# Rows by pair in pieces: the first tile's later batches and the second tile's parts moved into the second tile's routing

## The chip, the core and the metric

The kernel is one program on one core of a Trainium2 chip. The metric is device time in microseconds from one launch. The core has a tensor engine (PE), a vector engine (DVE), a scalar engine (ACT), a GpSimd engine (POOL, which here issues the gathers) and a sync engine (SP, which loads weights). Each runs its own list of instructions in the order in which they are written, and they meet at semaphores. Sixteen DMA engines move all data between HBM and SBUF.

## What is computed

A transformer block on x (256 tokens, width 1024), then two layers of a second kind on x and on a context of 256 tokens. What matters here is the feed-forward part of the second kind, which picks 16 experts per head for each token (8 heads, so 128 rows of each table per token):

```python
def chunk(hc):                                  # 128 tokens
    q = (hc @ w_query).reshape(128, 8, 2, 64)
    s = jnp.einsum('chpd,hpnd->chpn', q, sub_keys)
    s_top, i_top = lax.top_k(s, 16)             # 16 of 128, for each half
    cand = (s_top[:, :, 0, :, None] + s_top[:, :, 1, None, :]).reshape(128, 8, 256)
    best, pos = lax.top_k(cand, 16)
    eid = take_along_axis(cand_id, pos)         # 128 expert ids a token
    gate = softmax(best)
    u = jnp.take(u_tab, eid, axis=0)            # 128 rows of 1024 floats a token
    act = gelu(jnp.einsum('chkd,cd->chk', u, hc)) * gate
    v = jnp.take(v_tab, eid, axis=0)
    return jnp.einsum('chk,chkd->cd', act, v)
```

It runs for the context and x of the first layer and for x of the second: six tiles of 128 tokens.

## The kernel before

**Tiles.** Tiles 0 and 1 are the context (tag c0), 2 and 3 are x of layer 0 (x0), 4 and 5 x of layer 1 (x1). A tile is *routed*: `scores` (8 matmuls for each half, line 820) gives the scores, DVE finds the best in the steps "top 0" to "top 3", "pairs 0" to "pairs 3", "keys 0" to "keys 3" (`sixteen_best`, lines 1403 to 1415, and `route`), and the ids and gates are turned by PE (lines 836, 837) and copied (`experts`, semaphore `idx_ready`).

**Visits.** The tokens of a routed tile are worked off in pairs, 64 a tile, 384 in all, each by a `visit`. POOL gathers 128 rows of u and of v for both tokens of the pair (four indirect DMAs of half a MB, lines 2128 and 2138; three pairs of buffers each, u up to two pairs ahead). PE spreads the two tokens' own rows over all partitions (`spread`, four matmuls, line 425), DVE multiplies and sums (`dot`, two instructions, line 1035), ACT takes the gelu, DVE multiplies by the gate (line 1044), and two visits later PE adds the v rows (`outputs`, line 439). The spread needs the tile's rows in the form `hs`: a batch for eight pairs.

**Rows by pair.** To get `hs`, `hidden` transposes the tile's 128x1024 activations on PE (line 786), ACT and DVE split them into three bf16 parts (`hp1`, `hp2`, `hp3`; DVE lines 1438 and 1443, semaphore `parts_ready`), and `rows_by_pair` selects by matmul (line 799): eight batches, 12 matmuls each into one PSUM bank, which ACT copies to `hs`. The parts of one tile lie in one place, so those of the next wait until the rows before are made.

**What sets the order.** The order is written out by hand, the same on every engine. Work between visits is followed by `beat(key, us)`, which adds `us` to an account and puts in a visit for each 6.8 in it (PACE); `stream(key, upto)` puts in visits up to a number. The first stream of visits (0 to 255) opens after tile 0 is routed and runs through tile 1's routing, the whole first block, layer 0 of x, and ends in a tail of bare visits; the second (256 to 383) opens after tile 4's routing. While a stream is open, five of the eight PSUM banks belong to it and three are left for all other work. In `route_second("c0", BESIDE)` the first block's norm and first products (in1 0 and in1 1, line 403, 32 matmuls and two visits' beats each) stand between tile 1's routing steps.

`route_first` makes all eight batches of its tile after its routing. `route_second("c0")` then makes tile 1's parts and its eight batches, then its scores, then routes it; `route_second("x0")` and `("x1")` take the scores, route, and make parts and batches after the routing. In x0, two visits (`stream("tile 1 done")`) stand ahead of `route_second`.

## Time and profile before

| | us |
|---|---|
| median of 3 runs | 3563.71 |
| lowest, highest | 3562.61, 3567.37 |
| the profiled execution: its time | 3573.93 |
| its span (first to last instruction) | 3572.2 |
| busy: PE, DVE, POOL, ACT | 2369.1, 1678.6, 1485.1, 561.1 |
| moved by DMA | 1047.22 MB, mean 293 GB/s |

The profiled execution takes 10.2 us more than the median; times below are on its clock, from the start of its span. Stages: context mixer and tile 0's routing up to 448 us, tile 1's routing with the first products to 581, the first block to about 1160, layer 0 of x to 1545, tile 2's routing to 1608, tile 3's to 1746, the front of the layer-1 context and the tail of bare visits to 2410, layer 1 of x to 2740, tile 4's and 5's routing to 2903, the last tail to the end. Rows are read so: a row of the timeline has start, duration, engine, line, operation, output and input, how many instructions it merges, and in brackets how long the engine had been idle before and what it waited for.

### The profile page before, as it was taken

What the parts mean: (1) busy time and instruction counts of PE and PEld (TensorE: products, weight loads), DVE (VectorE), ACT (ScalarE), POOL (GpSimd) and SP (SyncE); (2) the same over time, 40 slices, a digit from 0 to 9 for tenths busy, and PEclk for the clock granted to TensorE, in tenths of its full rate; (3) what the DMA queues carried; (4) which work ended last, traced back from release to release, by engine and by line L of the source; (5) the groups of instructions that cost most, each with busy time, mean ns of one, the idle gap of its engine ahead of it and who ended that gap; (6) DMA issues with size and microseconds to landing.
All of it is one profiled execution on the core that took longest, in us unless ns stands there. A gap on an engine that the chain in (4) does not pass through costs nothing.

```text
span 3572.2 us, 36970 instructions
## 1 busy us (share of the span) xinstructions
PE 2369.1 (66%) x12540; PEld 1286.0 (36%) x12540; DVE 1678.6 (47%) x4368; ACT 561.1 (16%) x1180; POOL 1485.1 (42%) x1577
## 2 busy tenths in 40 slices
PE   6799657898998889964564444448996344444444
PEld 4477434366776446651110000006686110000000
DVE  2511655634334674376654444445415654444443
ACT  2310231401111252021220000003312110000000
POOL 1000034444444444405556666650000456666665
PEclk9899878799999979986665555558998555555555
DMA  8866669899999878938799999991140789999998
GB/s 291 320 241 231 229 223 327 297 358 364 371 361 362 292 274 320 367 121 292 281 344 361 355 352 355 360 340 61 54 170 25 249 315 354 356 355 360 356 354 322
DMA packets 325915, 1047.22 MB, mean 293 GB/s; under 512 B 27424, under 2 KB 38752, under 8 KB 325728
## 3 DMA queue, kind: packets, MB, share of 16 engines
q0 software_dynamic: 240192, 880.90, 66.4%
q1 hardware_dynamic: 85536, 163.95, 13.1%
q8 instruction: 101, 1.65, 0.2%
q14 instruction: 86, 0.70, 0.1%
HBM read 1043.70 MB, written 1.05 MB: 292 GB/s over the span
## 4 chain that ended last, share of the span: by engine, by line
PE 38%; DVE 20%; another core or an unknown queue 16%; issue 14%; DMA 4%; ACT 4%; PEld 3%; POOL 1%; DVEq 0%; PEldq 0%; ACTq 0%; POOLq 0%
PE ps L403 23%; DVE UV L1035 9%; PE ps L439 4%; PE ps L425 2%; PEld ps L403 2%; ACT arena L1661 2%; PE ps L395 2%; DMA UV<-in_v_tab,idxT 2%; PE ps L799 1%; DVE arena L1409 1%; DVE arena L1415 1%; DVE arena L1406 1%; DVE arena L1412 1%; PE ps L570 1%
## 5 line engine op out<-in xcount | busy, mean ns | idle before, releaser
L1035 DVE SCALAR_TENSOR_TENSOR UV<-ps,UV 128x1024 f32<-128x1024 f32 x768 | 909.7, 1222 | 1033.2 <-remote 594.2
L2128 POOL DMA_INDIRECT UV<-in_u_tab,idxT x768 | 724.4, 943 | 1296.7 <-DVE UV L1035 571.7
L2138 POOL DMA_INDIRECT UV<-in_v_tab,idxT x768 | 728.4, 948 | 395.0 <-issue 199.7
L439 PE MATMUL ps<-UV,acts 128*32 128x512 f32 x3072 | 637.9, 916 | 284.1 <-DMA UV<-in_v_tab,idxT 235.1
L403 PE MATMUL ps<-H,W 128*128 128x256 f32 (+2 forms) x3296 | 672.5, 365 | 44.5 <-ACT H L1661 22.8
L403 PEld LDWEIGHTS ps<-H,W 128*128 128x128 f32 (+1 forms) x3296 | 577.1, 195 | 159.9 <-issue 83.6
L425 PE MATMUL ps<-hs,selb 32*128 32x512 bf16 x1536 | 209.9, 532 | 610.1 <-DVE UV L1035 442.2
L425 PEld LDWEIGHTS ps<-hs,selb 32*128 32x128 bf16 x1536 | 42.3, 97 | 1068.2 <-DVE UV L1035 636.9
L403 PE MATMUL ps<-arena,W 128*128 128x256 f32 (+1 forms) x1632 | 373.0, 386 | 25.3 <-issue 13.7
L403 PEld LDWEIGHTS ps<-arena,W 128*128 128x128 f32 (+1 forms) x1632 | 305.3, 190 | 108.0 <-issue 57.7
L1661 ACT ACTIVATE gel<-dots 128x2 f32<-128x2 f32 x384 | 77.2, 202 | 1453.9 <-DVE UV L1035 883.4
L1661 ACT ACTIVATE arena<-ps 128x512 f32<-128x512 f32 (+6 forms) x288 | 150.6, 527 | 817.7 <-PE ps L403 646.5
L439 PEld LDWEIGHTS ps<-UV,acts 128*32 128x32 f32 x3072 | 76.0, 130 | 437.6 <-issue 435.4
L2108 POOL DMA_DIRECT2D UV<-in_w_mod x18 | 16.1, 899 | 254.9 <-ACTq L1713 254.0
L1184 DVE SCALAR_TENSOR_TENSOR arena<-arena,ps 128x512 f32<-128x512 f32 x44 | 30.2, 688 | 183.4 <-PE ps L403 179.2
L1661 ACT ACT_TABLE_LOAD x76 | 97.5, 1283 | 45.3 <-PE ps L570 24.4
L528 PE MATMUL ps<-UV,gateT 128*32 128x512 f32 x432 | 73.0, 647 | 26.5 <-DMA UV<-in_w_mod 14.3
L1262 DVE SCALAR_TENSOR_TENSOR arena<-arena,vec 128x256 f32<-128x256 f32 x180 | 79.3, 482 | 4.8 <-DVE arena L1016 0.7
L799 PE MATMUL ps<-arena,place 128*32 128x512 bf16 x576 | 51.9, 521 | 36.7 <-DVE arena L1443 20.1
L1044 DVE TENSOR_TENSOR acts<-gel,gateT 128x2 f32<-128x2 f32 x384 | 60.6, 158 | 6.3 <-ACT gel L1661 5.1
L1035 DVE DVE_READ_ACCUMULATOR UV<-ps,UV 128x1 f32 x768 | 63.5, 83 | 0.0
L1661 ACT ACTIVATE arena<-arena 128x512 f32<-128x512 f32 (+5 forms) x42 | 46.7, 1112 | 90.2 <-DVEq L1440 49.9
(198 smaller groups left out, 1639.1 us busy)
## 6 DMA issues: line engine op xcount, KB each, us to landing
W<-in_w_in SPq DMA_DIRECT2D x30, 2048.0 KB
UV<-in_w_mod POOLq DMA_DIRECT2D x18, 2048.0 KB, 12.8
W<-in_w_ff SPq DMA_DIRECT2D x16, 2048.0 KB
UV<-in_w_ada POOLq DMA_DIRECT2D x9, 2048.0 KB, 12.0
W<-in_w_out SPq DMA_DIRECT2D x8, 2048.0 KB
W<-in_w_mod POOLq DMA_DIRECT2D x6, 2048.0 KB, 17.6
W<-in_w_query SPq DMA_DIRECT2D x6, 2048.0 KB
UV<-in_u_tab,idxT POOLq DMA_INDIRECT x768
```

The lines of the kernel that those rows point to most:

```text
L395: last = mm(o, lhs[k], rhs[k], start=(k == 0), stop=(k == n - 1))
L403: last = mm(o, w[:, k, col:col + m], src[:, k, c], start=(k == 0), stop=(k == kt - 1))
L425: last = mm(ps[:, HB + r, :], selb[q, u:u + 1].to_broadcast([32, P]), hs[q, n % 2, s, :], start=True, stop=True)
L439: last = mm(ps[q:q + GROUP, YB, :], acts[:, tok % SLOTS, GROUP - 1 - r:2 * GROUP - 1 - r], Vs[:, tok % SLOTS, hf * 512:(hf + 1) * 512], st ...
L528: last = mm(o[q:q + 32, :], cond32[:, 4 * kh + kk, :], w[j][:, 4 * kh + kk, :], start=(kk == 0), stop=(kk == 3))
L799: last = mm(o[32 * r:32 * r + 32, :], place[:, at:at + 32], part[:, hf * 512:(hf + 1) * 512], start=(i == 0), stop=(i == 2))
L1035: dve.scalar_tensor_tensor(out=Us[:, j, :], in0=ps[:, b:b + 2, :].rearrange("p a b -> p (a b)"), scalar=1.0, in1=Us[:, j, :], op0=MUL, op1 ...
L1044: dve.tensor_tensor(out=acts[:, j:j + 2, GROUP - 1], in0=gel[:, j:j + 2], in1=gateT[:, n % 2, t:t + 2], op=MUL).then_inc(sem("acts"), 1)
L1262: last = dve.scalar_tensor_tensor(out=a, in0=u, scalar=wt, in1=a, op0=MUL, op1=ADD)
L1661: return act.activation(o, i, f, **kw)
L2128: pool.indirect_dma_start(Us[:, j, :], None, A["u_tab"], off).then_inc(sem(f"u_arrived{j}"), 16)
L2138: pool.indirect_dma_start(Vs[:, j, :], None, A["v_tab"], off).then_inc(sem(f"v_arrived{j}"), 16)
```

## The change

1. `rows_by_pair(n, batches)` makes only the batches that are named. `route_first` makes none any more. `route_second` makes batch 0 of the first tile, then scores 0 of the second, batch 1, scores 1, and batches 2 to 7 after step "top 0" of the second tile's routing.
2. In x0 the two visits "tile 1 done" stand behind these scores and no more ahead of the first tile's rows.
3. In c0 the second tile's `hidden` (transposes and parts) stands after "top 1", its rows after "top 2", behind the first block's norm, which moves from "top 0" to "top 2"; the first products in1 0 move from "top 2" to "top 3".
4. `rows_after(n)` makes the second tile's batches two at a time with a beat of 3.4 after each two; in x0 and x1 it takes the place of the eight batches in one piece.
5. The signals that the head sums are full are given ahead of the last beat in `mixer_front`; the instruction that carries the signal is the same.

Matmuls, copies and DMAs are the same in number and size.

```diff
@@ PE, the front of the mixer
                     if i:
                         last = key_sums(i - 1)
+                    if i == 4:
+                        full(last, (tag, "hsum"))
                     beat((tag, "hp", i), 2.5)
-                full(last, (tag, "hsum"))
...
@@ PE
-            def rows_by_pair(n):
+            def rows_by_pair(n, batches):
 
                 pe.wait_ge(sem("parts_ready"), n + 1)
-                for s in range(PAIRS // BATCH):
+                for s in batches:
...
                 routes(n)
                 for a in range(2):
                     give_back(("ht", n, a))
-                rows_by_pair(n)
 
             def route_second(tag, beside={}):
 
                 n = TILE_OF[tag] + 1
-                if tag == "c0":
-                    hidden(n, bank)
-                    rows_by_pair(n)
                 for a in range(2):
+                    rows_by_pair(n - 1, [a])
                     scores(n, a)
-                routes(n, beside)
+                if tag == "x0":
+                    stream("tile 1 done", max(seen[0], 2 * PAIRS + 2))
+                routes(n, {"top 0": [lambda: rows_by_pair(n - 1, range(2, 8))], **beside})
                 if tag != "c0":
                     hidden(n, bank)
-                    rows_by_pair(n)
+                    rows_after(n)
+
+            def rows_after(n):
+
+                for s in range(0, 8, 2):
+                    rows_by_pair(n, [s, s + 1])
+                    beat(("rows", n, s), 3.4)
...
-            BESIDE = {"top 0": [lambda: norm("f", "n1")], "top 2": [lambda: first_products(0)], "pairs 2": [lambda: first_products(1)]}
+            BESIDE = {"top 1": [lambda: hidden(1, bank)], "top 2": [lambda: norm("f", "n1"), lambda: rows_after(1)],
+                      "top 3": [lambda: first_products(0)], "pairs 2": [lambda: first_products(1)]}
...
             stream("tile 0 done", max(seen[0], PAIRS + 2))
             route_first("x0")
-            stream("tile 1 done", max(seen[0], 2 * PAIRS + 2))
             route_second("x0")
@@ DVE (ACT has the same moves)
-            BESIDE = {"top 0": [first_norm], "top 2": [lambda: first_products(0)], "pairs 2": [lambda: first_products(1)]}
+            BESIDE = {"top 1": [lambda: hidden_last(1)], "top 2": [first_norm, lambda: rows_after(1)],
+                      "top 3": [lambda: first_products(0)], "pairs 2": [lambda: first_products(1)]}
```

**PE, after tile 0 is routed.** Lines 836 and 837 (838, 839 after) turn its ids and gates; line 799 (801) makes rows, line 820 (822) the scores of tile 1, line 786 (788) the transposes, line 425 spreads, line 439 outputs, line 554 the norm's sum. Before:

```order
L837 MATMUL ps<-ident,arena 128x128
L799 MATMUL ps<-arena,place 32x512 x96
L786 MATMUL ps<-ident,H 128x128 x8
L799 MATMUL ps<-arena,place 32x512 x96
L820 MATMUL ps<-arena 128x128 x8
L425 MATMUL ps<-hs,selb 128x512 x4
L820 MATMUL ps<-arena 128x128 x8
L425 MATMUL ps<-hs,selb 128x512 x4
L554 MATMUL ps<-H,ones 128x256 x8
```

After:

```order
L839 MATMUL ps<-ident,arena 128x128
L801 MATMUL ps<-arena,place 32x512 x12
L822 MATMUL ps<-arena 128x128 x8
L801 MATMUL ps<-arena,place 32x512 x12
L822 MATMUL ps<-arena 128x128 x8
L425 MATMUL ps<-hs,selb 128x512 x4
L801 MATMUL ps<-arena,place 32x512 x72
L788 MATMUL ps<-ident,H 128x128 x8
L425 MATMUL ps<-hs,selb 128x512 x8
L439 MATMUL ps<-UV,acts 32x512 x4
L554 MATMUL ps<-H,ones 128x256 x8
```

The scores of tile 1 had 192 row matmuls ahead of them and now have 12; the first spread now has 24 ahead. Tile 1's own 96 row matmuls come behind the norm, in two blocks of 48 with a visit behind each.

**DVE, the same place.** Lines 1438 and 1443 (1445, 1450 after) make a tile's parts, 1403 to 1415 (1410 to 1422) are a "top" step, 1035 (1042) the dots of a visit. Before:

```order
L1438 TENSOR_TENSOR arena<-ps,arena 128x512 x2
L1443 TENSOR_TENSOR arena<-arena 128x1024
L1438 TENSOR_TENSOR arena<-ps,arena 128x512 x2
L1443 TENSOR_TENSOR arena<-arena 128x1024
L1035 SCALAR_TENSOR_TENSOR UV,dots<-ps,UV 128x1024 x2
L1403 MAX arena<-arena 128x8 x4
```

After:

```order
L1445 TENSOR_TENSOR arena<-ps,arena 128x512 x2
L1450 TENSOR_TENSOR arena<-arena 128x1024
L1410 MAX arena<-arena 128x8 x4
L1413 MAX_INDEX arena<-arena 128x8 x4
L1416 MATCH_REPLACE arena<-arena 128x128 x4
L1419 MAX arena<-arena 128x8 x4
L1422 MAX_INDEX arena<-arena 128x8 x4
L1042 SCALAR_TENSOR_TENSOR UV,dots<-ps,UV 128x1024 x2
```

Tile 1's first step stood behind its parts and the first visit, and stands ahead of both now. Its parts come two steps later.

**PE, after tile 5 is routed.** The same lines; the stream of visits goes on behind. Before:

```order
L786 MATMUL ps<-ident,H 128x128 x8
L425 MATMUL ps<-hs,selb 128x512 x4
L439 MATMUL ps<-UV,acts 32x512 x4
L799 MATMUL ps<-arena,place 32x512 x96
L425 MATMUL ps<-hs,selb 128x512 x4
```

After:

```order
L788 MATMUL ps<-ident,H 128x128 x8
L425 MATMUL ps<-hs,selb 128x512 x4
L439 MATMUL ps<-UV,acts 32x512 x4
L801 MATMUL ps<-arena,place 32x512 x24
L425 MATMUL ps<-hs,selb 128x512 x4
L439 MATMUL ps<-UV,acts 32x512 x4
L801 MATMUL ps<-arena,place 32x512 x48
L425 MATMUL ps<-hs,selb 128x512 x4
L439 MATMUL ps<-UV,acts 32x512 x4
L801 MATMUL ps<-arena,place 32x512 x24
```

Two visits now stand inside the block of rows. After tile 3 it is two blocks of 48 with a visit behind each. Of the 256 visits of the first stream, numbers 0 to 15 (before 0 to 13) now fall before tile 1 is routed, each later place in the first block and in layer 0 of x has a number higher by two, and the last two such places (the last `out` product and the norm behind it) have none; 150 visits (before 149) are done when the front of the layer-1 context begins.

## Rows read from the trace of the kernel before

**Rows 1.** Windows of long stretches: busy us (instructions) of each engine, PEclk, DMA share, GB/s
```profile
700.00:1140.00 440.00, 416.73 (x2163) 304.29 (x2162) 166.38 (x348) 44.79 (x111) 198.52 (x212) 0.98 0.98 363
...
1630.00:1744.00 114.00, 44.07 (x228) 8.09 (x232) 86.84 (x315) 11.41 (x25) 68.13 (x72) 0.52 0.90 326
...
2799.00:2903.00 104.00, 40.28 (x194) 6.93 (x194) 82.83 (x298) 10.52 (x21) 60.60 (x63) 0.50 0.87 314
...
2930.00:3572.00 642.00, 273.75 (x1312) 38.33 (x1312) 268.58 (x568) 24.05 (x111) 399.40 (x426) 0.51 0.94 352
```
**Rows 2.** The same view of five short stretches, at the blocks of rows
```profile
464.00:482.00 18.00, 10.91 (x136) 5.53 (x136) 5.02 (x8) 9.44 (x16) 0.37 (x1) 0.81 0.01 4
...
1624.00:1632.00 8.00, 4.47 (x43) 2.04 (x44) 6.18 (x13) 3.33 (x7) 3.75 (x4) 0.97 0.46 137
...
1762.00:1776.00 14.00, 10.13 (x80) 4.51 (x68) 4.85 (x8) 7.82 (x13) 1.88 (x2) 0.87 0.13 41
...
2790.00:2799.00 9.00, 4.40 (x40) 3.03 (x40) 3.67 (x12) 4.81 (x8) 1.35 (x2) 0.61 0.08 31
...
2916.00:2925.00 9.00, 7.44 (x60) 1.71 (x52) 3.96 (x8) 3.32 (x7) 1.88 (x2) 0.68 0.30 102
```
**Rows 3.** Timeline after tile 0's routing: PE, DVE and POOL (columns: section on the profile)
```profile
452.78 6.40 PE L799 MATMUL ps<-arena,place 128*32 128x512 bf16 x72 [5.00 <-DVE arena L1443]
...
469.76 7.61 PE L799 MATMUL ps<-arena,place 128*32 128x512 bf16 x96 [5.06 <-DVE arena L1443]
...
465.61 0.69 DVE L1438 TENSOR_TENSOR arena<-ps,arena 128x512 f32<-128x512 f32 x1 [12.88 <-ACT arena L1661]
...
468.48 1.22 DVE L1443 TENSOR_TENSOR arena<-arena 128x1024 bf16<-128x1024 f32 x1 [1.27 <-ACT arena L1661]
...
481.88 0.87 DVE L1403 MAX8 arena<-arena 128x8 f32<-128x128 f32 x4
...
481.63 0.93 POOL L2128 DMA_INDIRECT UV<-in_u_tab,idxT  x1 [21.88 <-DVE UV L1035]
```
**Rows 4.** Timeline of tile 1's routing: DVE, then the two first products on PE
```profile
490.11 0.42 DVE L1016 TENSOR_SCALAR varb<-ps 128x256 f32<-128x256 f32 x1 [0.35 <-DVE gs L1128]
...
501.47 0.86 DVE L1403 MAX8 arena<-arena 128x8 f32<-128x128 f32 x4
...
506.81 0.87 DVE L1403 MAX8 arena<-arena 128x8 f32<-128x128 f32 x4
...
525.54 1.22 DVE L1035 SCALAR_TENSOR_TENSOR UV<-ps,UV 128x1024 f32<-128x1024 f32 x1 [7.98 <-PE ps L425]
...
535.81 1.15 DVE L1456 TENSOR_TENSOR arena<-arena 128x512 f32<-128x512 f32 x2
...
503.72 7.82 PE L403 MATMUL ps<-H,W 128*128 128x256 f32 x32
...
516.45 8.28 PE L403 MATMUL ps<-H,W 128*128 128x256 f32 x32
```
**Rows 5.** Timeline, DVE in the norm at the end of layer 0 of x
```profile
1537.77 1.22 DVE L1035 SCALAR_TENSOR_TENSOR UV<-ps,UV 128x1024 f32<-128x1024 f32 x1 [0.31 <-DVE varb L1016]
```
**Rows 6.** Timeline after tile 2's routing: PE, then DVE
```profile
1611.75 4.70 PE L799 MATMUL ps<-arena,place 128*32 128x512 bf16 x60 [5.00 <-DVE arena L1443]
...
1622.74 1.23 DVE L1035 SCALAR_TENSOR_TENSOR UV<-ps,UV 128x1024 f32<-128x1024 f32 x1 [11.04 <-PE ps L425]
...
1634.51 0.87 DVE L1403 MAX8 arena<-arena 128x8 f32<-128x128 f32 x4 [0.24 <-DVE X L1053]
```
**Rows 7.** Timeline after tile 3's rows: POOL's next gather
```profile
1773.58 0.94 POOL L2128 DMA_INDIRECT UV<-in_u_tab,idxT  x1 [14.88 <-DVE UV L1035]
```
**Rows 8.** Timeline after tile 4's routing: PE, then DVE
```profile
2779.18 7.21 PE L799 MATMUL ps<-arena,place 128*32 128x512 bf16 x75 [5.00 <-DVE arena L1443]
...
2797.59 0.87 DVE L1403 MAX8 arena<-arena 128x8 f32<-128x128 f32 x4
```
**Rows 9.** Timeline after tile 5's rows: POOL's next gather
```profile
2922.58 0.94 POOL L2128 DMA_INDIRECT UV<-in_u_tab,idxT  x1 [8.62 <-DVE UV L1035]
```

More of the change, by code:

```diff
@@ L1636, in _ @@
             route_first("x0")
-            beat("tile 1 done")
             route_second("x0")
@@ L1995, in route_first @@
                 second_part(n)
-                rows_by_pair(n)
             def route_second(tag, beside={}):
@@ L2083, in _ @@
             route_first("x0")
-            beat("tile 1 done")
             route_second("x0")
```

49 lines of the change are left out of this document (30 added, 19 removed).

## The prediction, made before the changed kernel was run

> **What bounds the kernel now.** I read the windows of long stretches first. In the last tail the DMA engines are busy for 0.94 of the time at 352 GB/s, and POOL issues 426 gathers in 642 us: at four a pair, 106.5 visits of 6.03 us [rows 1]. A visit moves 2.1 MB, so this stretch is bound by the gathers, with PE at 43%. The first block (700 to 1140) is full on both sides, PE 95% busy and DMA 0.98 [rows 1]. While a tile is routed beside a stream, DMA stands at 0.90 and 0.87 and DVE is busy for 76 to 80% of the time; a visit takes 6.3 and 6.6 us [rows 1]. So after an `idx_ready` that opens gathers, any time in which the DMA engines stand still is paid in full. Then I looked for such time, in short windows: 18 us after tile 0's routing with a DMA share of 0.01, 8 us at 0.46 after tile 2's, 14 us at 0.13 after tile 3's rows, 9 us at 0.08 after tile 4's, 9 us at 0.30 after tile 5's rows [rows 2]. All five are at blocks of rows. The timeline says why: POOL has issued what its buffers hold and waits for the dots of the first pair, 21.88 us at the first place, 14.88 and 8.62 us at the third and the last [rows 3, 7, 9]; those dots wait for PE, 11.04 us after tile 2 [rows 6].
>
> **Place 1, tile 1's routing.** The removed time: tile 0's parts are ready at 452.78, and DVE starts tile 1's "top 0" only at 481.88 [rows 3]. Between the end of the second block of rows (469.76 + 7.61 = 477.4) and that start lie the scores, two copies and one visit's dots (two of 1.2 us, 2.4); so scores and copies are 2.1 us, and a batch is 7.61/8 = 0.95 us [rows 3]. After the change "top 0" starts at 452.8 + 0.95 + 2.1 = 456, which is 26 us earlier. Most of it is given back, because the same DVE and PE work comes behind it in another order. I walk it: a top step is 506.81 - 501.47 = 5.3 us [rows 4]; top 0 to 461.3, visit 0 to 463.7, top 1 to 469.0; tile 1's parts as before, 465.61 to 469.70, 4.1 us [rows 3], to 473.1; visit 1 to 475.5; top 2 to 480.8; visit 2 to 483.2; the norm with two visits in it 501.47 - 490.11 = 11.4 us [rows 4], to about 495. Then two blocks of 48 row matmuls with a visit behind each. PE needs 3.8 us a block, but with three banks the fourth batch waits until ACT has finished scaling the norm's output; I put both visits, with DVE waiting for PE in between, at 12.5 us (bounds 4.8, the dots alone, and 16), to 507.5. Now top 3 runs beside the first of the two products, which takes 7.8 us, and the second takes 8.3 [rows 4]: PE gives the spread behind the first at 515.5, DVE is free at 518, the spread behind the second comes at 525, and visits 8 and 9 are done at 531. Before, this point (the start of "pairs 0") was at 535.81, after a wait of 7.98 us for the same product [rows 4]. So 26 us become 5, with ten visits done where there were eight. From there to the end of the first block nothing moves against anything, each place only has a visit number two higher, so the 5 us stay. At the end of layer 0 of x the last two places have no visit: one of them stood inside the norm, between the mean and the reciprocal [rows 5], 2.4 us of dots, the other lay partly under a wait for PE; together 3 us. Place 1 gives **8 us** (bounds -7, if the products are slow as in the second rival, and +15, if the two blocks of rows hide).
>
> **Place 2, tiles 2 and 3.** The rows start at 1611.75 and the first dots at 1622.74, "top 0" after three visits at 1634.51 [rows 6]. After: batch 0 and half the scores, dots from about 1615, visit 128 to 1617.5, visit 129, whose u rows are gathered behind four other gathers, to about 1623 (a guess between 1620 and 1625), top 0 to 1628.4, visit 130 and the adding of a filled group of outputs to 1632.8 (before, three visits and this adding took 1634.51 - 1622.74 = 11.8 us, which leaves some 2 us for it beside waits). The same state before is 1634.51 + 5.3 = 1639.8. So 7 us, while the hole in the DMA is 8 x 0.54 = 4.3 us [rows 2]; I take 7, since in this stretch DVE is nearly as full as the DMA (bounds 4.3 and 11). Batches 2 to 7 then need 5.7 us of PE, which lies under DVE's steps; uncovered it would hold the next spread and cost these 5.7 us. After tile 3, the hole of 14 x 0.87 = 12.2 us [rows 2] now has two visits in it. They keep the gathers going and put PE's next norm back by some 3 us for spreads and outputs; about 6 us of the hole are won (bounds 2 and 10). Place 2 gives **13 us**. By the other count it is the same: routing ends with one visit fewer and 7 + 2.4 earlier, two visits in the rows cost 3 of it, and the tail is one visit (6.0) shorter: 12.4.
>
> **Place 3, tiles 4 and 5.** Rows start at 2779.18, "top 0" at 2797.59 behind one visit [rows 8]. After: two batches and two sets of scores with their copies, 2 x (0.95 + 2.1) = 6.1 us, visit 256 with its spread 3 us, top 0 at about 2788.5: 9 us earlier, against a hole of 9 x 0.92 = 8.3 [rows 2]. I take 8.5 (bounds 8 and 10). After tile 5 the hole is 9 x 0.70 = 6.3 us [rows 2] and POOL's wait 8.62 [rows 9]; with a visit after two batches and one after six POOL goes on; 6 us (bounds 2 and 8). What follows is the tail alone, so nothing takes it back. Place 3 gives **14.5 us**.
>
> **The earlier signals** in the front of the mixer are set by the same matmul; 0 us. A turn-back of outputs can now fall beside them; one costs at most some 2 us once.
>
> **Sum.** 8 + 13 + 14.5 = 35.5 us. The profiled execution took 3573.93 and would take 3538.4; the median of the runs is 10.2 lower, and 3563.7 - 35 = **3529 us**.
>
> **A rule weighed.** PE runs the start of the row blocks after a wait and at a mixed clock: the short windows over them show 0.61 to 0.87, between 1.2 GHz (0.50) and 2.4 GHz (1.00), and the tail 0.51 [rows 1, 2]. The change cuts blocks of 96 matmuls into 12, 72 and 48. The Trainium skill, "TensorE: Matmul & The Clock Gate", section "Why this matters for your kernels", says to keep matmuls in long bursts without gaps, since the engine goes back to its lower clock; by that rule this change works against itself. By the rows a block of 96 is 7.61 us or somewhat more, and where it lies under DVE a slower one costs nothing; so the sum above stands, and what the rule could take is the first rival below.
>
> **Rivals.** (a) *The clock takes place 1 back.* If the two first products run at 1.2 GHz, since the row blocks before them are broken up, each takes up to twice its 7.8 and 8.3 us. Nearly all of the first's surplus hides under top 3 and visit 7, the second's does not: 8 to 12 us. With that, place 1 is about -4, and with the lower bounds of the two others (6 and 10) the sum is 12 to 16: about 3549. For it: the two take 7.82 and 8.28 us already, so neither ran wholly at one clock. Against it: rows now stand right ahead of them. (b) *More stays than I think.* If the blocks of rows after the norm hide and DVE is not held by the products, place 1 gives 15, place 2 17 and place 3 18: 50 us, 3514. Against it: PE's order is fixed, and DVE did wait for this product. (c) *Banks: slower.* Before, the 16 batches of tiles 0 and 4 had all eight banks, since the stream was not open; now 14 of them follow its opening and share three banks with scores, transposes and products, and ACT empties them between its gelus, in its own order. A batch that waits for a bank holds the spread behind it on PE, and so the dots and the gathers. If each of the 16 held the stream by more than 35/16 = 2.2 us, the gain would be gone, and at 3.5 us, two copies behind a gelu with its table, it would be 3563.7 + 21 = 3585. Against it: ACT is the least busy engine (561.1 us in all), and tile 1's rows ran at 0.95 us a batch on three banks already [rows 3]. (d) *No gain: the bytes bind.* If the gathers were bound throughout, starting them earlier would change nothing: 3563. Against it: the holes [rows 2].
>
> **How the numbers follow.** The forecast has 0.70, (a) 0.12, (b) 0.10, (c) 0.04, (d) 0.04. The forecast's own range comes from the bounds, which do not all fall on one side: 3515 to 3545. To take in (a) and half of (b) and to leave out no more than 2 in 10, I give 3513 to 3552. 0.2% is about what a measurement of this kernel can tell from no change, 7.1 us, so faster means below 3556.6: all of the forecast, (a) and (b), 0.92; the same 0.04, slower 0.04.
>
> **What would show it.** In the profile after: tile 1's "top 0" at 456 and "pairs 0" at 531 (a later one than 536 means that (a) or (c) holds); the windows with a DMA share near nothing gone after tiles 4 and 5, POOL's waits of 14.88 and 8.62 us down to 5 or less; the end of tile 1's routing 5 us earlier, of layer 0 of x 8 us, of the first stream 21 us, of tile 5's routing 30 us. It would be wrong if PE, held in a block of rows for a bank, were named as what the dots wait for, or if the tail's pace were not 6.0 us a visit.

## Result and the profile after

| | before | after |
|---|---|---|
| median of 5 runs each, us | 3564.99 | 3538.61 |
| lowest, highest | 3562.61, 3567.37 | 3533.62, 3546.55 |
| the profiled execution | 3573.93 | 3546.23 |
| its span | 3572.2 | 3544.5 |

The ratio is 0.9935, with a 95% interval of 0.9922 to 0.9948: the kernel is 23 us faster (18.5 to 27.8), the medians differ by 26.4, the two profiled executions by 27.7. The forecast was a gain of 35, at 3529; the measured 3538.6 lies 9.6 us above it, inside the range of 3513 to 3552. Line numbers of DVE and POOL have moved: 1035 is 1042, 1403 is 1410, 2128 is 2151, 1498 (the copy of the ids, just ahead of `idx_ready`) is 1505, ACT's 1661 is 1677.

The short windows with the least DMA in the trace of after, as long as those in [rows 2] (columns as there). The last line stands behind the opening of the stream after tile 4:

```profile
465.00:483.00 18.00, 7.85 (x77) 2.66 (x74) 16.17 (x71) 10.20 (x17) 6.52 (x7) 0.74 0.49 164
...
1603.00:1611.00 8.00, 3.00 (x22) 1.50 (x24) 3.10 (x5) 1.66 (x2) 4.62 (x5) 0.50 0.49 135
...
1740.00:1754.00 14.00, 10.40 (x120) 3.46 (x120) 6.86 (x13) 5.72 (x11) 4.81 (x6) 0.75 0.45 159
...
2760.00:2769.00 9.00, 3.86 (x36) 2.32 (x40) 3.07 (x5) 2.01 (x3) 6.02 (x6) 0.50 0.56 172
...
2898.00:2907.00 9.00, 6.45 (x68) 1.63 (x64) 5.10 (x11) 3.22 (x8) 4.06 (x5) 0.85 0.53 183
...
2784.00:2793.00 9.00, 2.69 (x20) 0.31 (x12) 8.10 (x38) 1.08 (x4) 4.70 (x5) 0.72 0.76 246
```

Three holes are smaller and still there: behind tile 0's ids the share of 0.01 has become 0.49, behind tile 3's 0.13 has become 0.45, and behind tile 5's 0.30 has become 0.53. The windows at 1603 and 2760 are of another kind. They hold the moment at which gathering begins (tile 2's ids are there at 1603.68, tile 4's at 2759.98), which stands empty in both kernels. Behind it the hole after tile 4 has gone: the least share of a window that starts between 2762 and 2800 us is 0.76, where before had 0.08. After tile 2 it is 0.58 (1637 to 1645, at the last four batches), and later stretches of the same routing reach 0.59 in both kernels; before had 0.46 in [rows 2], and 0.37 one us ahead of it.

The timeline of tile 1's routing, DVE and then PE. DVE's "top 0" starts at 460.52, and "pairs 0" at 532.22:

```profile
460.52 0.88 DVE L1410 MAX8 arena<-arena 128x8 f32<-128x128 f32 x4 [5.29 <-ACTq L1979]
...
504.84 1.23 DVE L1042 SCALAR_TENSOR_TENSOR UV<-ps,UV 128x1024 f32<-128x1024 f32 x1 [5.49 <-remote]
...
526.90 1.23 DVE L1042 SCALAR_TENSOR_TENSOR UV<-ps,UV 128x1024 f32<-128x1024 f32 x1 [5.79 <-PE ps L425]
...
532.22 1.15 DVE L1463 TENSOR_TENSOR arena<-arena 128x512 f32<-128x512 f32 x2
...
509.03 7.17 PE L403 MATMUL ps<-H,W 128*128 128x256 f32 x32
...
519.28 7.17 PE L403 MATMUL ps<-H,W 128*128 128x256 f32 x32
```

The windows over the two first products, of after and then of before (columns as in [rows 1]):

```profile
509.00:516.00 7.00, 7.00 (x36) 6.00 (x32) 6.13 (x29) 0.77 (x2) 5.17 (x7) 1.00 0.87 294
...
519.00:526.00 7.00, 7.00 (x34) 5.95 (x32) 2.12 (x5) 0.34 (x2) 3.75 (x4) 1.00 0.80 276
```

```profile
503.70:511.50 7.80, 7.80 (x36) 6.50 (x32) 7.56 (x47) 0.00 (x0) 1.58 (x2) 0.91 0.75 266
...
516.40:524.70 8.30, 8.30 (x40) 6.84 (x36) 1.15 (x3) 0.00 (x0) 5.63 (x6) 0.86 0.92 328
```

The table gives, for both pairs of traces (a second pair was taken on another chip, below), how much later (+) or earlier (-) the kernel after passes a point than the kernel before, in us. Each point is the start of a DVE row (line 1498 or 1505; for the first tail, the norm of x behind it).

| point | first pair | second pair | forecast |
|---|---|---|---|
| tile 0's ids | +2.5 | -2.2 | 0 |
| tile 1's ids | -3.2 | -7.6 | -5 |
| tile 2's ids | -3.1 | -5.9 | -8 |
| tile 3's ids | -12.2 | -14.5 | -17.4 |
| behind the first tail | -14.4 | -12.4 | -21 |
| tile 5's ids | -23.9 | -21.5 | -30 |
| end | -27.7 | -23.8 | -35.5 |

Nothing that the change touches stands ahead of tile 0's ids, but for the earlier signals; +2.5 and -2.2 show how far two traces of the same stages differ. The gain of place 1 is therefore counted from tile 0's ids below.

### The profile page after: what moved, and what is told of

Its sections match the earlier page's. It is cut to its first block, busy times and chain, and to the rows that moved or that the text cites. A ratio compares the mean times of both kernels' runs of the same rounds, so it can differ in the third digit from the quotient of the medians.

```text
span 3544.5 us, 36981 instructions
## 1 busy us (share of the span) xinstructions
PE 2371.6 (67%) x12540; PEld 1285.4 (36%) x12540; DVE 1678.7 (47%) x4368; ACT 559.0 (16%) x1179; POOL 1487.4 (42%) x1577
## 3 DMA queue, kind: packets, MB, share of 16 engines
q8 instruction: 101, 1.65, 0.2%
## 4 chain that ended last, share of the span: by engine, by line
PE 37%; DVE 20%; another core or an unknown queue 17%; issue 14%; DMA 5%; ACT 3%; PEld 2%; POOL 1%; DVEq 0%; PEldq 0%; ACTq 0%; POOLq 0%
PE ps L403 24%; DVE UV L1042 9%; PE ps L439 4%; PE ps L425 3%; PEld ps L403 2%; ACT arena L1677 2%; PE ps L395 2%; DMA W<-in_w_mod 1%; DMA UV<-in_v_tab,idxT 1%; DVE arena L1422 1%; DVE arena L1413 1%; PE ps L528 1%; DVE arena L1416 1%; PE ps L801 1%
## 5 line engine op out<-in xcount | busy, mean ns | idle before, releaser
L1212 DVE SCALAR_TENSOR_TENSOR X<-ps,half,X 128x256 f32<-128x256 f32 x32 | 14.0, 479 | 99.8 <-PE ps L403 91.0
```

## Experiments

All medians, in us, beside runs of the kernel before on the same chip. Chips differ: between 3000 and 3300 us, in the bare tail, the gathers move 355 to 361 GB/s on those of after, e5 to e9 and p1 ("the slower chips"), and 409 on the one of e1 to e4 ("the faster chip"), so only differences and ratios are compared. Part 5 of the change, the earlier signals, stands in every kernel of this table; it was not tested alone.

| kernel | this | before | difference | ratio, 95% interval |
|---|---|---|---|---|
| after2 | 3536.14 | 3560.47 | -24.3 | 0.9930, 0.9917 to 0.9942 |
| e1: place 1 alone | 3362.96 | 3369.89 | -6.9 | 0.9978, 0.9968 to 0.9987 |
| e2: places 2 and 3 alone | 3349.20 | 3369.89 | -20.7 | 0.9943, 0.9926 to 0.9960 |
| e3: rows in one piece | 3352.04 | 3369.89 | -17.9 | 0.9952, 0.9935 to 0.9968 |
| e4: tile 1's rows late | 3338.26 | 3369.89 | -31.6 | 0.9904, 0.9885 to 0.9923 |
| e5: e4, products split | 3531.25 | 3560.47 | -29.2 | 0.9920, 0.9908 to 0.9933 |
| e6: e5, first visit early | 3526.27 | 3560.47 | -34.2 | 0.9900, 0.9884 to 0.9916 |
| e7: e6 without the split | 3531.77 | 3558.50 | -26.7 | 0.9917, 0.9900 to 0.9933 |
| e8: e7, rows inside all routings | 3528.36 | 3558.50 | -30.1 | 0.9911, 0.9889 to 0.9932 |
| p1: after, lists shifted | 3535.27 | 3558.50 | -23.2 | 0.9929, 0.9915 to 0.9944 |
| e9: e6, a batch a visit | 3526.66 | 3561.16 | -34.5 | 0.9905, 0.9886 to 0.9924 |

### e1 and e2: the places apart

e1 keeps `route_first` and `route_second` of before for x0 and x1 (the edits here are against after, and shortened; the two visits "tile 1 done" stand ahead again):

```diff
                 for a in range(2):
                     give_back(("ht", n, a))
+                if tag != "c0":
+                    rows_by_pair(n, range(8))
@@ route_second, x0 and x1
-                routes(n, {"top 0": [lambda: rows_by_pair(n - 1, range(2, 8))], **beside})
-                hidden(n, bank)
-                rows_after(n)
+                routes(n, beside)
+                hidden(n, bank)
+                rows_by_pair(n, range(8))
```

> The change at the first place alone (tile 0's rows and tile 1's routing); tiles 2 to 5 as in the kernel before. Theory (the places add up, and this one is worth 8 us by the prediction, 3 to 6 by the trace of after): 3557 to 3561 as a median, 3 to 8 us under before; tile 1's idx_ready 5 to 6 us earlier, and the end of the front of layer 0 of x still 4 us earlier. In the trace of after some 3.5 us of this are lost between 1223 and 1537 us. If the moved visit numbers lose them, the same loss stands here, and tile 2's idx_ready comes only 0 to 3 us earlier than before. Rival (the loss belongs to nothing that the change does at this place, a clock or a load that differs from run to run): tile 2's idx_ready comes 6 us or more earlier here.

e2 does the opposite, with c0 and BESIDE as before (the part in `route_second`):

```diff
+                if tag == "c0":
+                    hidden(n, bank)
+                    rows_by_pair(n, range(8))
+                    for a in range(2):
+                        scores(n, a)
+                    routes(n, beside)
+                    return
```

> The change at the second and third places alone (tiles 2 to 5); tile 0's rows, tile 1's parts and rows and the first products stand as before. Theory: 3534 to 3541 as a median, 23 to 30 us under before; nothing moves up to 1600 us but for 1 us of noise, tile 3's idx_ready 9 us earlier, end of the first tail 11 us, tile 5's idx_ready 20 us, the end 24 us. Rival (all of the gain hangs together, tile 1's earlier routing leaves a state on which the later ones rest): less than 20 us under before.

Measured: -6.9 and -20.7, together -27.6, beside -26.4 and -24.3 for the whole change on other chips: the places add up within the noise. No trace of before is from this chip; since e1 has place 1 alone and e2 has all but place 1, each serves as the other's baseline. The copies of tile 1's and of tile 2's ids, first e1, then e2, and last tile 5's for both:

```profile
573.37 0.28 DVE L1510 TENSOR_SCALAR idxT<-ps 128x128 uint32<-128x128 f32 x1
...
1583.94 0.29 DVE L1510 TENSOR_SCALAR idxT<-ps 128x128 uint32<-128x128 f32 x1 [0.84 <-PE ps L839]
...
2770.66 0.29 DVE L1510 TENSOR_SCALAR idxT<-ps 128x128 uint32<-128x128 f32 x1 [2.08 <-PE ps L839]
```

```profile
575.35 0.28 DVE L1513 TENSOR_SCALAR idxT<-ps 128x128 uint32<-128x128 f32 x1
...
1591.38 0.29 DVE L1513 TENSOR_SCALAR idxT<-ps 128x128 uint32<-128x128 f32 x1 [0.84 <-PE ps L839]
...
2759.03 0.29 DVE L1513 TENSOR_SCALAR idxT<-ps 128x128 uint32<-128x128 f32 x1 [2.13 <-PE ps L839]
```

Against e2, e1 stands at -2.0 at tile 1's ids and at -7.4 at tile 2's, so the stretch between them gives 5.4 us here. By e1's expectation that is the rival: the moved visit numbers are not what lost 3.5 us in the trace of after. But it is one trace, and e3, which has the same order in this stretch, gains only 0.2 on e2 in it. How e1 and e3 come apart can be seen: e3 falls back by 3.8 us between 835 and 1132 us. One window of e3 and then of e1 in it (columns as in [rows 1]):

```profile
1060.00:1070.00 10.00, 7.75 (x41) 3.77 (x41) 5.78 (x12) 0.41 (x2) 4.26 (x5) 0.83 0.99 368
```

```profile
1060.00:1070.00 10.00, 7.75 (x48) 4.96 (x49) 5.78 (x12) 0.41 (x2) 5.30 (x6) 1.00 1.00 374
```

PE is busy in both, the granted clock is 0.83 in e3 and 1.00 in e1, and 41 matmuls are done for 48. That such dips explain the 3.5 us in the trace of after was not shown.

### e3: the second tile's rows in one piece

```diff
                 for s in range(0, 8, 2):
                     rows_by_pair(n, [s, s + 1])
-                    beat(("rows", n, s), 3.4)
+                    if n == 1:
+                        beat(("rows", n, s), 3.4)
```

> The changed kernel, but the rows of tiles 3 and 5 in one piece behind their routing, without visits between them, as in the kernel before. Theory (a visit within the rows is worth 6 us at each of the two, as predicted): 12 us more than after, POOL's waits behind the rows back at 14 and 8 us. Rival, from the trace of after (at tile 5 the stall of PE and ACT in the middle of the rows, with DVE waiting 8.90 us, is there with and without visits in between): 5 to 8 us more than after, most of it at tile 3 and 2 us or less at tile 5.

Measured: -17.9, which is 9.7 us above the -27.6 that e1 and e2 make together; after itself did not run on this chip. Between the two expectations, and the split over the places is the rival's: against e2, e3 loses 7.5 us between tile 3's ids and the end of the first tail, and from tile 5's ids to the end 1.4. On this chip POOL waits 9.83 us behind tile 3's rows in one piece, and in e2, with two visits in them, no gather of u rows from 1701 to 1730 waits more than 0.31:

```profile
1722.54 0.94 POOL L2154 DMA_INDIRECT UV<-in_u_tab,idxT  x1 [9.83 <-DVE UV L1043]
```

```profile
1712.32 0.94 POOL L2168 DMA_INDIRECT UV<-in_u_tab,idxT  x1 [0.31 <-DVE UV L1050]
```

How large the holes are on this chip is seen in e1, where the rows behind tiles 3 and 5 and those of tile 4 stand as before. Its windows with the least DMA there, and then e2's over the same 14 us:

```profile
1721.00:1735.00 14.00, 8.87 (x41) 5.18 (x41) 9.29 (x15) 6.12 (x11) 4.08 (x4) 0.74 0.38 126
...
2674.00:2683.00 9.00, 1.89 (x24) 1.20 (x24) 6.59 (x30) 3.74 (x6) 3.74 (x4) 0.83 0.46 153
...
2786.00:2795.00 9.00, 3.05 (x28) 0.52 (x24) 7.36 (x15) 0.66 (x4) 6.87 (x8) 0.87 0.89 296
```

```profile
1721.00:1735.00 14.00, 9.88 (x44) 5.45 (x43) 10.79 (x19) 7.23 (x13) 9.78 (x10) 0.77 1.03 409
```

Against the tail's 1.03 they are short of 9.1, 5.1 and 1.3 us. Over the stretches in question e2 gains 5.9, 5.4 and 1.8 us on e1: on this chip the two later holes are worth what the windows say, the first about two thirds of it.

### e4: tile 1's rows, and the 26 us

```diff
-            BESIDE = {"top 1": [lambda: hidden(1, bank)], "top 2": [lambda: norm("f", "n1"), lambda: rows_after(1)],
-                      "top 3": [lambda: first_products(0)], "pairs 2": [lambda: first_products(1)]}
+            BESIDE = {"top 1": [lambda: hidden(1, bank)], "top 2": [lambda: norm("f", "n1")],
+                      "top 3": [lambda: first_products(0)], "pairs 2": [lambda: first_products(1)], "keys 0": [lambda: rows_after(1)]}
```

> The changed kernel, with tile 1's rows moved from behind the first norm (step top 2) to step keys 0 of tile 1's routing; its transposes and parts stay at top 1. Theory (what takes 26 us of earlier start back is DVE's waiting for PE, which makes the rows and both first products in one stretch): pairs 0 at about 518 us with eight visits done, tile 1's idx_ready 7 to 10 us earlier than in after, and the median 6 to 9 us under after. Rival (DVE is full with its own work there, or the rows at keys 0 hold the spreads just as long): tile 1's idx_ready within 2 us of after, and the median too.

Measured: -31.6, 4 us under the sum of e1 and e2. "pairs 0" starts at 518.21, as expected, with eight visits done, where e1 has it at 526.94 with ten. In e4, DVE's two largest waits around it are for the spreads behind the second half products:

```profile
512.89 1.23 DVE L1042 SCALAR_TENSOR_TENSOR UV<-ps,UV 128x1024 f32<-128x1024 f32 x1 [5.97 <-PE ps L425]
...
518.21 1.15 DVE L1463 TENSOR_TENSOR arena<-arena 128x512 f32<-128x512 f32 x2
...
536.61 1.23 DVE L1042 SCALAR_TENSOR_TENSOR UV<-ps,UV 128x1024 f32<-128x1024 f32 x1 [3.88 <-PE ps L425]
```

Of the 8.7 us at "pairs 0" against e1, 4.9 are left at tile 1's ids and 2.6 at tile 2's; a large part of the 8.7 is the dots of the two visits that now come later (four of 1.2 us). The size is between the two expectations. That rows right behind the norm hold DVE through PE is shown, at some 5 us of the 21 that were taken back; the rest belongs to the other work of the walk.

### after2 and before2: the pair again

> The changed kernel itself once more, beside a run of the kernel before on the same chip. Theory (the three places add up, and where they are does not depend on the chip): 26 to 29 us under before, as e1 and e2 add up to (6.9 + 20.7). The size of places 2 and 3 goes with the time of a visit: on a chip whose tail moves 409 GB/s the holes are worth less at the start of a tail and as much elsewhere. Rival (part of the gain of one place depends on another): less than 22 or more than 33.

> The kernel before, unchanged, to have its trace from the same chip as the others. Expected: the time of the comparison runs; if the gathers of this chip run at 409 GB/s, the wait of POOL behind tile 5's rows is 2 to 3 us where the first chip had 8.62, and if they run at 352 GB/s, a stall of ACT inside the block of tile 5's rows is there again.

Measured: -24.3, and 3560.90 for before2. So the 26.4 of the first comparison, the 24.3 here and the 27.6 of e1 and e2 together agree within their intervals. On this chip (tail at 359 GB/s in both) a stall of ACT inside tile 5's rows is there again in before2, 2.98 us; more of it under p1.

### e5 and e6: split products, and an early first visit

e5 sets one half of a first product behind each of four steps; e6 adds one visit in x1:

```diff
-                      "top 3": [lambda: first_products(0)], "pairs 2": [lambda: first_products(1)], "keys 0": [lambda: rows_after(1)]}
+                      "top 3": [lambda: half_product(0, 0)], "pairs 0": [lambda: half_product(0, 1)],
+                      "pairs 1": [lambda: half_product(1, 0)], "pairs 2": [lambda: half_product(1, 1)], "keys 0": [lambda: rows_after(1)]}
@@ route_second (e6)
                     scores(n, a)
+                    if a == 0 and tag == "x1":
+                        stream(("first", n), seen[0] + 1)
+                        owed[0] -= PACE
```

> The kernel of e4, with the four halves of the first two products set singly behind the steps top 3, pairs 0, pairs 1 and pairs 2 instead of two behind top 3 and two behind pairs 2. In e4 DVE waits 5.97 and 3.88 us for the spreads behind the two second halves. Theory (these waits are what holds place 1): both are down to 1 us or less, tile 1's idx_ready comes 5 to 9 us earlier than in e4 and the end as much. Rival (the wait moves: each half product stands ahead of a spread, and a pairs step of 3.6 us doesn't cover a half product of 7.2 us, so DVE waits 2 to 3 us at each of three places instead): within 2 us of e4.

> The kernel of e5, and in layer 1 of x the first visit of the second stream stands behind the first set of scores and ahead of the second batch and the second set. Theory (while the stream opens, the gathers stand still, so what delays the first dots is paid in full): DVE's wait for them drops from 7.3 to 4 us, tile 5's idx_ready and the end come 3 us earlier than in e5. Rival (the dots then only wait for the rows of u, or top 0 is put off as much): within 1 us of e5.

Measured for e5: -29.2. The waits are 2.54, 5.50 and 3.29 us at three places for 5.97 and 3.88 at two, so the rival holds: the wait has moved. Their sum is 11.3 us for 9.9, on another chip.

```profile
515.31 1.23 DVE L1054 SCALAR_TENSOR_TENSOR UV<-ps,UV 128x1024 f32<-128x1024 f32 x1 [2.54 <-PE ps L425]
...
528.47 1.23 DVE L1054 SCALAR_TENSOR_TENSOR UV<-ps,UV 128x1024 f32<-128x1024 f32 x1 [5.50 <-PE ps L425]
...
536.92 1.23 DVE L1054 SCALAR_TENSOR_TENSOR UV<-ps,UV 128x1024 f32<-128x1024 f32 x1 [3.29 <-PE ps L425]
```

Measured for e6: -34.2. DVE's wait for the first dots of tile 4 is 4.00 us, and 8.44 in e5. Between tile 4's and tile 5's ids it takes 3.2 us less than e5, as the theory says; the medians differ by 5.0 us and the intervals overlap, so the time alone doesn't show it. Against after2, on the same chip, e6 is 9.9 us faster, with intervals that do not overlap (up to 0.9916, and from 0.9917).

### p1: where the shortfall lies

On the slower chips PE makes rows slowly in one place. In the trace of after it makes the second part of tile 5's rows so (PE, then ACT's copy, DVE's next dots and POOL's next gather):

```profile
2889.65 0.38 PE L801 MATMUL ps<-arena,place 128*32 128x512 bf16 x1 [0.25 <-issue]
...
2890.38 0.38 PE L801 MATMUL ps<-arena,place 128*32 128x512 bf16 x1 [0.35 <-issue]
...
2897.53 1.47 PE L801 MATMUL ps<-arena,place 128*32 128x512 bf16 x12 [2.95 <-ACTq L1683]
...
2896.84 0.60 ACT L1677 ACTIVATE hs<-ps 128x512 bf16<-128x512 f32 x1 [8.32 <-remote]
...
2899.67 1.22 DVE L1042 SCALAR_TENSOR_TENSOR UV<-ps,UV 128x1024 f32<-128x1024 f32 x1 [8.90 <-PE ps L425]
...
2901.72 0.94 POOL L2151 DMA_INDIRECT UV<-in_u_tab,idxT  x1 [6.21 <-DVE UV L1042]
```

A block of 48, which takes 2.77 us at tile 3's rows in e2, stops after 25 matmuls and goes on one by one every 0.72 us. ACT copies a batch only after standing for 8.32 us, with no releaser named ("<-remote" is a signal that the trace can't put down to an engine of this core); PE then waits 2.95 us for the bank that ACT frees, and the spread, DVE and POOL wait behind PE. p1 shifts the instruction lists, by 128 instructions on PE and 64 on ACT:

```diff
+                for _ in range(128 if n == 0 else 0):
+                    pe.drain()
                 pe.wait_ge(sem("routed"), nxt("routed"))
@@ ACT, behind tile 0's routes
+                for _ in range(64 if n == 0 else 0):
+                    act.sem_inc(sem("pool_paced"), 1)
```

> The changed kernel with 128 drains put into PE's list and 64 semaphore increments into ACT's, both at a place where these engines wait (the end of tile 0's routing). Nothing else moves. On the chips with a tail at 355 GB/s both profiles of after show the same thing inside tile 5's rows: matmuls of line 801 one by one every 0.72 us, and ACT idle for 8.3 us ahead of the third copy, with no releaser named; before it 3.0 us. Theory (the instructions themselves come late there, since the engines' lists are fetched in blocks by the same DMA engines, and a block's border lies at this place): with the lists shifted by half a block, the slow matmuls and the 8.3 us go away from this place, the end comes 3 to 6 us earlier than in after, or they turn up elsewhere and the time stays. Rival (it belongs to this piece of the program, to banks, semaphores or the clock): the same slow matmuls and a wait of ACT of about 8 us at the same copy. On a chip at 409 GB/s neither is expected to show anything.

Measured: -23.2, and ACT's wait is 7.64 us at the same copy, as the rival says:

```profile
2883.11 0.41 PE L801 MATMUL ps<-arena,place 128*32 128x512 bf16 x3 [0.30 <-issue]
...
2884.54 0.43 PE L801 MATMUL ps<-arena,place 128*32 128x512 bf16 x3 [1.01 <-issue]
...
2889.55 0.60 ACT L1679 ACTIVATE hs<-ps 128x512 bf16<-128x512 f32 x1 [7.64 <-remote]
```

The DMA rows name packets of two queues as instruction loads, q8 and q14. The one on q8 came at 2881 to 2883 in after2, right at the stall, and at 2891 to 2893 in p1, behind it; the stall stayed at the rows. p1, with 128 instructions more on PE, has 102 loads on q8 for 101, so this is taken to be PE's queue, and the stall isn't a border of PE's list: there my theory fell. Loads on q14 are not ruled out: they came within the us from 2888 and from 2896 in after, from 2882 and 2891 in after2 and from 2888 in p1, all in the stall or at its end (ACT's late copies start at 2896.84, 2891.11 and 2889.55). Which engines' lists they are, and whether they cause the stall or follow it, no run shows.

The Trainium skill, "Runtime: NRT & Kernel Launch", section "Instruction fetch mechanics", says that an engine fetches its next block of 16 KiB over its own DMA queue while it runs the current one, mostly hidden. On q8 the trace of after agrees in size (101 loads, 1.65 MB), and in p1 the stall did not follow its border; on q14 the loads are half as large (86, 0.70 MB).

### e7 and e8: rows inside every routing

e7 is e6 with the first products in pairs again. e8 does in x0 and x1 what c0 does:

```diff
-                routes(n, {"top 0": [lambda: rows_by_pair(n - 1, range(2, 8))], **beside})
                 if tag != "c0":
-                    hidden(n, bank)
-                    rows_after(n)
+                    beside = {"top 1": [lambda: hidden(n, bank)], "keys 0": [lambda: rows_after(n)]}
+                routes(n, {"top 0": [lambda: rows_by_pair(n - 1, range(2, 8))], **beside})
```

> The kernel of e6 without the split of e5: tile 1's rows at step keys 0, both halves of each first product together as in after, and the first visit of the second stream behind the first set of scores. Theory (the split only moved waits, and the rows at keys 0 bring some 5 us): between after and e6, 32 to 35 us under before. Rival (the split is worth 3 us or more): 3 us or more above e6, under 31 us below before.

> The kernel of e7, and in both layers of x the second tile's transposes and parts stand behind its step top 1 and its rows behind keys 0, inside its routing, as they do for tile 1. So no block of rows stands behind the routing of tiles 3 and 5. Theory (each stop of the gathers behind those rows is paid in full; on a chip with a tail at 355 GB/s the changed kernel has POOL waiting 9.2 us for the dots in front of tile 3's rows and 6.2 us inside tile 5's): 6 to 14 us under e7; on a chip at 409 GB/s 2 to 8 us. Rival (DVE, which is busy for 8 tenths of the routing, takes it back, since its 4 us of parts and two visits more stand in it now, and the spreads wait for the rows at keys 0): within 3 us of e7.

Measured for e7: -26.7, which by the numbers is the rival (the split would be worth more than 3 us), but e6 and e7 ran on different chips and their intervals overlap, so this is unclear. Measured for e8: -30.1, 3.4 us under e7, between its two expectations, with single runs from 3512 to 3536; this is unclear too. Its trace shows that the stop has not gone. At keys 0 of tile 5 (PE, ACT, DVE):

```profile
2850.03 0.42 PE L801 MATMUL ps<-arena,place 128*32 128x512 bf16 x3 [0.22 <-issue]
...
2858.53 0.60 ACT L1680 ACTIVATE hs<-ps 128x512 bf16<-128x512 f32 x1 [12.52 <-remote]
...
2861.37 1.22 DVE L1044 SCALAR_TENSOR_TENSOR UV<-ps,UV 128x1024 f32<-128x1024 f32 x1 [13.07 <-PE ps L425]
```

The stall has moved with the rows, and is longer. It stands at tile 1's rows as well: where these are at keys 0, on the slower chips (e5 to e9), DVE waits 6.25 to 6.31 us for the dots behind the row matmuls, each time; e4, on the faster chip, has no such wait there.

### e9: a batch a visit

```diff
+                if n > 1:
+                    for s in range(8):
+                        rows_by_pair(n, [s])
+                        stream(("rows", n, s), seen[0] + 1)
+                    return
```

> The kernel of e6, with the rows of tiles 3 and 5 made one batch at a time, 12 matmuls, and one visit behind each of the eight (e6 has 24, a visit, 48, a visit, 24, and after tile 3 twice 48 with a visit behind each). On the chips with a tail at 355 GB/s each block of 48 beside running gathers shows matmuls of line 801 one by one after 24 to 33 of them and ACT standing for 5 to 8 us, wherever the block stands (12.5 us in e8 at keys 0 of tile 5); p1 showed that it is not a border of the instruction lists. Theory (it is the length of the burst of row matmuls): with 12 in a piece PE and ACT don't stand at all there, DVE's largest wait for a spread behind them is 3.5 us, as in the bare tail, POOL's wait below 2 us, and the median lies 5 to 10 us under e6, 40 to 45 us under before. Rival (each batch beside running gathers costs the same, however they are cut): eight waits of 1 us or more above the tail's, and a time within 3 us of e6. On a chip at 409 GB/s no stall is expected in either, and 2 to 4 us under e6 for the time that POOL no longer waits behind tile 3's rows.

Measured: -34.5, as e6. The long run of single matmuls is gone and the DMA is nearly full over the whole of tile 5's rows; windows of e9, and of the shorter stretch of e6:

```profile
2868.00:2924.00 56.00, 31.03 (x212) 7.17 (x216) 25.48 (x52) 6.65 (x18) 35.33 (x39) 0.65 0.97 358
```

```profile
2868.00:2900.00 32.00, 20.64 (x160) 4.94 (x156) 14.20 (x28) 6.94 (x15) 19.76 (x22) 0.71 0.91 328
```

ACT still takes up finished batches late, though. This one is done at 2895.6 and is copied at 2902.97 (PE, then ACT):

```profile
2894.05 1.53 PE L801 MATMUL ps<-arena,place 128*32 128x512 bf16 x12
...
2902.97 0.60 ACT L1700 ACTIVATE hs<-ps 128x512 bf16<-128x512 f32 x1 [9.03 <-remote]
```

DVE's waits behind the batches are still up to 5.5 us, where the theory had 3.5. From tile 5's ids to the end, e9 gains 4.9 us on before2 and e6 0.2, in single traces on different chips; the medians don't show it. So the theory has only the form of the burst right; the late copy, and the time, are the rival's. The stall does not need a burst of 48.

## Why the prediction was right or wrong

**The bound.** Right. The last tail runs at 353 GB/s with a DMA share of 0.94 in after (2930 to 3540 us) and at 352 and 0.94 before [rows 1], and what moved the end were the holes of [rows 2]. On the faster chip the parts of the change together give 27.6 us, much as elsewhere, though a visit takes 5.2 us there (232 gathers in 300 us, last section).

**Place 1, the walk.** Right to the size: 26 us earlier [rows 3] become 5.7, 5.4 and 4.6 us at tile 1's ids (first pair, second pair, e1 against e2), each measured from tile 0's ids; 5 was forecast. "pairs 0" was put at 531 and stands at 532.22, which is 81.9 us behind tile 0's ids where 83.2 was forecast. Within it two terms were off and a third made up for them, so that this closeness is in part luck. "top 0" comes 10.2 us behind tile 0's ids in both traces of after, not 8.2; the first batch alone took PE 1.47 us, where 0.95 was put. From the norm's end to "top 3" I took 12.5 us, bounds 4.8 and 16; DVE is free of the norm at 496.7 and starts "top 3" at 512.13, 15.4 us, with a wait of 5.49 for the first spread. In e1, at 409 GB/s, "top 3" starts at 507.13, where the walk had it. Behind it the products ran shorter, 7.17 us each for 7.8 and 8.3 [rows 4], and DVE waited 5.79 us for the second, for 7.98 before. e4 shows that the blocks of rows behind the norm are one of the things that take the 26 us back: without them tile 1's ids come 4.9 us earlier.

**Rival (a), and the rule weighed.** Neither came about. With the row blocks cut up ahead of them the two first products take 7.17 us, less than before, and the granted clock over them is 1.00, the level of 2.4 GHz, in both, where before had 0.91 and 0.86. PE had its row blocks and spreads ahead of them in either kernel; the pieces did not cost it the clock.

**Place 1, the 3 us at the end of layer 0.** Between tile 1's and tile 2's ids the two pairs lose 0.1 and 1.7 us, and against e2 the kernels with place 1 gain 5.4 (e1) and 0.2 (e3). Traces scatter by more than the term here, so it is neither confirmed nor refuted; it is 3.1 of the 5.3 us that are missing in the first pair (counted from tile 0's ids), and 4.7 of 13.9 in the second.

**Place 2.** The first half is right: 9.1, 8.6 and, e2 against e1, 7.8 us at tile 3's ids for 9.4. "top 0" stands behind two visits, and the batches 2 to 7 lie under DVE's steps. The second half is the one that fell short. It was to give the rest of 13, which is 3.6, and by the end of the first tail it gave 2.2 in the first pair and -2.1 in the second; on the faster chip it gives 5.9 to 7.5 (e2 against e1 and e3). The step that failed is "They keep the gathers going": it held on the faster chip, where no wait of POOL's inside these rows is over 0.31 us, and not on the slower ones. There POOL's wait of 14.88 us is not down to 5; it stands ahead of the rows now, 9.20 us, with 3.15 in them (13.31 in before2, and 7.13 and 3.09 in after2). PE, ACT, DVE and POOL there, in after:

```profile
1728.78 1.59 PE L788 MATMUL ps<-ident,H 128*128 128x128 f32 x8
...
1738.14 1.08 ACT L1677 ACTIVATE arena<-ps 128x512 bf16<-128x512 f32 x2 [12.07 <-remote]
...
1733.94 0.29 DVE L1505 TENSOR_SCALAR idxT<-ps 128x128 uint32<-128x128 f32 x1 [4.87 <-remote]
...
1744.82 0.94 POOL L2151 DMA_INDIRECT UV<-in_u_tab,idxT  x1 [9.20 <-DVE UV L1042]
```

The transposes end at 1730.4 by the profile, and ACT takes them up only at 1738.14. It looks like the stall of p1 in another place: an engine takes PE's finished bank late, 7.8 us here and 3.0 in after2, beside running gathers, with no releaser named.

The stall is not all of it. The window in the hole has won 14 x (0.45 - 0.13) = 4.5 us in the first pair and 14 x (0.59 - 0.19) = 5.6 in the second, near the 6 that the prediction had. What is left of this at the end of the tail depends on the tail. The table gives how much earlier the first gather of a visit starts, all in the bare tail, where the change touches nothing:

| visit | first pair | second pair | e2 against e1 |
|---|---|---|---|
| 170 | -8.9 | -16.7 | -7.5 |
| 200 | -12.1 | -14.8 | -6.8 |
| 230 | -12.9 | -9.4 | -6.4 |
| 255 | -14.2 | -12.0 | -6.4 |

On the slower chips two traces drift against each other by 5 to 7 us within one tail; on the faster chip by 1. So 2.2 and -2.1 do not size the term, and how much of it the stall took stays open.

**Place 3.** The first half is right: 9.5 and 9.1 us for 8.5 (5.4 on the faster chip, where the hole in e1 is 5.1 us and not 8.3). The second was to give 6 and gives 3.8 and 2.3, and 1.4 to 1.8 on the faster chip. Two reasons are seen. On the slower chips the stall of p1, 8.3 us in after where before had 3.0, stands in the rows, and POOL still waits 6.21. And I sized the hole from the first chip's [rows 2, 9], in which such a stall of ACT was already contained: on the faster chip, without it, POOL waits 2.30 to 2.62 us behind the same rows in one piece (e3, e1), and the hole is 1.3 us, so there was little to win.

**Banks, rival (c).** The sign that the prediction gave for being wrong is there in after: PE, in tile 5's rows, waits 2.95 us for a bank, and DVE's 8.90 us are put down to PE's spread behind it. So the queue of waits was the one of rival (c), which had 0.04. But ACT was not at its gelus, it stood, for 12.07 and 8.32 us at two places, and did not take 3.5 us at sixteen; the loss of rival (c) did not come.

**The sum.** Of 35.5 us, the first halves and the walk (5 + 9.4 + 8.5 = 22.9) came as forecast, with 24.3 in the first pair and 23.1 in the second. The three later terms, 3 + 3.6 + 6 = 12.6, gave 5.9 in the first pair and -1.5 in the second. That is where the 9 us between the forecast and the measured gain lie; each of the three is within the scatter of single traces, so only their sum is shown to be too high. On the faster chip the total is much the same and its parts are others: the walk and the first halves give 4.6 + 7.8 + 5.4 = 17.8, the two second halves 5.9 + 1.8, and the end of layer 0 something between 0.2 and 5.4. That the gain is nearly the same on both kinds of chip is thus in part chance.

## What to carry to other kernels

Where a queue of transfers is the bound, look for the short windows in which it stands, and move what stands ahead of the first consumer; such a gain (here 5 to 9 us a place) was forecast within 1 us from rows of the same chip, and to some 3 us for a faster one. A gain that comes from work put *between* running transfers can be worth less than the hole says: before you price it, see whether the hole itself contains a stall, since that stall may stay. Look at a long stretch that the change doesn't touch, too: if two traces drift in it by 5 us, terms of 3 us can't be read behind it. When work of an early start only changes its order on two full engines, walk it step by step; here 21 of 26 us were taken back, and some 5 of these could be had by moving one block once more (e4).

## What was not expected of the hardware

**Two speeds of the same tail.** Between 3000 and 3300 us the same gathers move 355 to 361 GB/s on the first chip and three later ones, with a DMA share of 0.95 to 0.96, and 409 on the chip of e1 to e4, with 1.03; a whole run takes 3370 us there and 3560 elsewhere. Windows of 300 us in the last tail of e9 and of e1:

```profile
3000.00:3300.00 300.00, 128.47 (x616) 17.59 (x616) 129.12 (x268) 11.18 (x53) 190.39 (x204) 0.50 0.95 355
```

```profile
3000.00:3300.00 300.00, 145.43 (x708) 21.21 (x704) 145.49 (x306) 12.76 (x60) 217.37 (x232) 0.51 1.03 409
```

The Trainium skill, "DMA: Bandwidth & Descriptors", section "Where 436 GB/s comes from", gives about 358 GB/s as the HBM limit of a core, half of a stack that two cores share, and says that in transfers between HBM and SBUF this side binds. The slower chips lie within 1% of it. The one at 409 does not, so there it doesn't bind a single core; whether it is what holds the slower ones no run shows.

**The late bank.** Only on the slower chips ACT stands long at blocks of rows beside running gathers. In tile 5's rows it stands for 3.0 us in both traces of before, 7.6 to 8.3 in after, after2 and p1, 6.6, 4.8 and 6.9 in e5, e6 and e7, up to 9.0 in e9, and 12.5 in e8, where they stand elsewhere. In most of these no releaser is named, and PE's batch was done before; in e6 and e7 the wait is put down to PE's slow matmuls. It stays at its rows when PE's and ACT's lists are shifted, moves with them when they are moved, and is there with bursts of 12 matmuls as with 48. What holds it, the memory, the semaphores, the instruction loads of q14, or the recording itself, is open.
